# Squares of two feature blocks added on Pool ahead of the product with ones, in a norm of a two-layer decoder kernel

## The chip, the cores and the metric

The kernel runs on the 8 cores of one Trainium2 chip as one program. Times are device microseconds (us) of the slowest core. Each pair of cores takes one of four prompt sequences: the even core takes the first half of its tokens and 64 sample tokens, the odd core the second half with a halo of 136 tokens. The two kinds run differently built programs, and an even core ends last.

## The reference

One inference step of a trunk of two layers, for 4 prompts of 2048 tokens and 32 samples of 8 tokens, model width 2048. Cut to what matters here:

```python
def rmsnorm(x, g):
    r = lax.rsqrt(jnp.mean(xf * xf, axis=-1, keepdims=True) + EPS)
    return (xf * r).astype(x.dtype) * g

for i in range(2):
    h = rmsnorm(x, norm_mix[i])
    # token mixer (layer 0: gated short convolution, layer 1: sliding window attention)
    # in parallel with cross-attention into 256 memory tokens
    x = x + concat([mixer(h), cross_attention(h, mk, mv)]) @ w_out[i]
    x = x + swiglu(rmsnorm(x, norm_ffn[i]), w_gate[i], w_up[i], w_down[i])
y = rmsnorm(x, norm_final)
```

The changed code is the sum of squares in `rmsnorm`, over the 2048 features of a token.

## The kernel before

Activations lie transposed in SBUF: features on the 128 partitions in 16 blocks c = 0 to 15, tokens along the free dimension, cut into three tiles of 288 to 400 tokens. `xT` (tensor sb_rx, f32) is the residual stream; sb_ra and sb_rb are two bf16 buffers, sb_rc is shared by slots and temporaries, sb_rs holds five weight slots, sb_rn the temporaries of norms.

A mean over features is a sum over partitions, so TensorE makes it. `Norm.square(c)` squares one block of one token tile on ScalarE into a bf16 buffer, and `Norm.ones` multiplies that buffer by a 128x128 matrix of ones (sb_onesb), summing over the 16 blocks in one PSUM bank. `root` makes the inverse root on ScalarE (Ln, Exp); `apply(c)` scales block c on VectorE (STT, line 445). Six square buffers rotate and the product of block c is issued at `stat(c + 3)`; the last four products come at c = 15.

Norms of `xT` run in these places. In `l0_first` (layer 0's first norm) `norm(0)` runs alone while `xT` arrives by DMA; `norm(1)` and `norm(2)` are lists of side work, of which `qm(ti)` issues 0, 4, 6 and 7 pieces behind its four groups h = 0 to 3 of 16 matmuls. In a `sweep` (in `pass2`, where a group has 6 matmuls, and in the last `down` of each FFN, where it has 8) each of 16 groups d of a token tile is followed by `add_x` (VectorE, line 439, PSUM into `xT`) and by `stat(d)`, and the 16 `apply` of the tile before (`pending`) run one behind each of d = 0 to 7 and two behind d = 8 to 11. There are four sweeps of three tiles. One more norm is that of the memory tokens (`mem0_norm`).

Every engine runs its instructions in the order in which the Python code emits them. Pool (GpSimd) issues the DMAs of all weights, in order of use: before item i of the program its loads are emitted as far as slots are free. Line 1295 makes the loads 2 to 8 wait for a part of `xT`, numbers 7 and 8 for the last quarter of tile 1:

```python
while qi < len(queue):
    ...
    if s.free >= i:
        break
    DMA("pool", [(v.ap, src)], xT.r((12, 16), TA[0] if qi < 7 else TA[1]) if 2 <= qi < 9 else [], v.r(), s.key)
```

Line 451 lets at most eight (`PQD`) of Pool's DMAs be in flight: each waits for the landing of the one eight before it. Pool also scales the softmax rows in attention (line 442).

Of the kernel before, what the change touches and what calls it, by code (L numbers as in the profile page):

```python
# [296 lines left out]
def build():  # L297
# [46 lines left out]
    RS = Reg(chip, "rs", 5 * 4096, gran=4096)  # L344
    RN = Reg(chip, "rn", 2 * 800 + 2 * 1600 + 1024, gran=32)
    RK = Reg(chip, "rk", 1664, gran=32)
# [12 lines left out]
    def half(odd):  # L359
# [9 lines left out]
        sq = [View(RN, 800 * i, (400,), BF16) for i in range(2)]  # L369
        sqf = sq + [View(RC, 15360 + 800 * i, (400,), BF16) for i in range(4)]  # L370
        sqx = sq + [View(RC, 800 * i, (400,), BF16) for i in range(4)]
        rr = [View(RN, 1600 + 1600 * i, (400,), F32) for i in range(2)]
# [12 lines left out]
        stg0 = [View(RC, o, (256,), F32) for o in (23552, 24576, 9664)]  # L385
        sqm = sq + [View(RC, 27648 + 800 * i, (400,), BF16) for i in range(2)]
        sg = [View(RC, 1600 * i, (400,), F32) for i in range(2)]
        hmem1 = View(RA, 26752, (16, 256), BF16)
        mstage = [View(RA, 34944 + 1024 * i, (256,), F32) for i in range(2)]
        stg1 = [View(RC, 7424 + 1024 * i, (256,), F32) for i in range(3)]  # L390
        NB = 8 + odd
# [88 lines left out]
        common = [Slot(RS, 4096 * i, "w%d" % i) for i in range(5)]  # L480
        xslots = [Slot(RC, o, "w%d" % (5 + i if i < 4 else 23)) for i, o in enumerate((3328, 15360, 19456, 23552, 27648))]
        aslots = [Slot(RA, 4096 * i, "w%d" % (9 + i)) for i in range(6)]
# [26 lines left out]
        class Norm:  # L509
            def __init__(self, src, gi, dst, a, b, bufs=sqx):  # L510
                self.src, self.gi, self.dst, self.a, self.b, self.n = src, gi, dst, a, b, b - a
                self.bufs, self.lag = bufs, len(bufs) // 2
                self.q = []
                self.bt = None
                self.k = None

            def square(self, c):
                if self.bt is None:
                    self.bt, self.br = bank("N")
                s = self.bufs[nsq[0] % len(self.bufs)]  # L520
                nsq[0] += 1
                ACTF(s.ap[:, :self.n], self.src.ap[:, c, self.a:self.b], AF.Square, self.src.r(c, (self.a, self.b)), s.r((0, self.n)))
                self.q.append((c, s))

            def ones(self):
                c, s = self.q.pop(0)
                MM(self.bt[:, :self.n], onesb[:], s.ap[:, :self.n], c == 0, c == 15, s.r((0, self.n)) + ["onesb"], [self.br])

            def stat(self, c):
                self.square(c)  # L530
                while len(self.q) > (self.lag if c < 15 else 0):
                    self.ones()

# [274 lines left out]
        def l0_first(slots):  # L808
# [4 lines left out]
            def norm(ti):  # L813
                nm = Norm(xT, 0, bigA, TA[ti][0], TA[ti][1], sqf)
                side.extend([lambda c=c: nm.stat(c) for c in range(16)] + [lambda: nm.root(next_rr())] + [lambda c=c: nm.apply(c) for c in range(16)])
# [132 lines left out]
        def mem0_norm(_):  # L948
            nm = Norm(memT, 5, hmem0, 0, 256, sqm)
            side.extend([lambda c=c: nm.stat(c) for c in range(16)] + [lambda: nm.root(rmem)] + [lambda c=c: nm.apply(c) for c in range(16)])  # L950
            rate[0] = 3
# [495 lines left out]
```

How the kernel before makes its waits and increments, by code:

```python
    def run(self, eng_name, eh, esem, dsem):  # L97
        ops = self.ops
        waited = {}
        for o in ops:
            if o["eng"] != eng_name:
                continue
            need = {}
            for j in o["deps"]:
                p = ops[j]
                key = ("d", p["dma"]) if p["dma"] is not None else ("e", p["eng"])
                if p["sv"] > need.get(key, 0):
                    need[key] = p["sv"]
            for key, v in need.items():
                if waited.get(key, 0) >= v:
                    continue
                waited[key] = v
                sem = dsem[key[1]] if key[0] == "d" else esem[key[1]]
                eh.wait_ge(sem, v)
            if o["fn"] is None:
                continue
            ins = o["fn"](eh)
            if o["dma"] is not None:
                if not isinstance(ins, (list, tuple)):
                    ins = [ins]
                assert len(ins) == o["ndma"], (len(ins), o["ndma"])
                for x in ins:
                    x.then_inc(dsem[o["dma"]], 16)
            elif o["sig"]:
                ins.then_inc(esem[eng_name], 1)
```

## Time and profile before

| | |
|---|---|
| median of 3 runs | 2915.32 us (2914.01 to 2915.5) |
| the profiled execution | 2913.25 us |
| its span, slowest core (core 2) | 2911.7 us |
| spans of the even cores | 2909.0 to 2911.7 us |
| spans of the odd cores | 2867.1 to 2871.7 us |
| TensorE busy | 2829.2 us (97%), 18868 matmuls |
| VectorE, ScalarE, Pool busy | 952.7, 510.9, 396.0 us |
| granted TensorE clock | 0.993 of full speed |

A matmul's record lasts longer than its turn: in a full queue one of 368 columns starts every 0.156 us, while its row says 0.32. The busy share of an engine is a mean over stages, so the rows further down are taken from the stages in which a norm runs.

### The profile page before, as it was taken

How to read it: one execution, taken by the hardware profiler on the slowest of the kernel's cores; microseconds unless marked ns; L12 is line 12 of the kernel's file. 1: busy time of each engine (PE TensorE's matmuls, PEld its weight loads, DVE VectorE, ACT ScalarE, POOL GpSimd, SP SyncE). 2: the span in 40 equal slices, each digit the busy share in tenths (PEclk: the TensorE clock that was granted, in tenths of full speed). 3: DMA queues.
4: the chain of work that ended last, by engine and by line, in shares of the span. 5: the costliest groups of instructions: out<-in, count | busy, mean ns of one | idle time of the engine just before them, and what ended most of it. 6: DMA issues, size and time to landing. Idle time of an engine off the chain costs nothing.

```text
span 2911.7 us, 51081 instructions; the slowest of 8 cores (2867.1 to 2911.7 us)
## 1 busy us (share of the span) xinstructions
PE 2829.2 (97%) x18868; PEld 1780.1 (61%) x18868; DVE 952.7 (33%) x2004; ACT 510.9 (18%) x1410; POOL 396.0 (14%) x700
## 2 busy tenths in 40 slices
PE   6999999999999999999999899999999999999997
PEld 3665666666666666666656545566666666666664
DVE  2425436331302113131162568544131221312116
ACT  3213203100010000000133666220000000000013
POOL 0013111000000100001002667100000010000100
PEclk9999999999999999999999999999999999999999
DMA  8485447344352642525324412734317254252513
GB/s 191 90 131 84 74 69 123 73 81 89 83 100 51 122 75 51 90 41 102 51 44 82 81 31 46 122 59 87 73 21 122 48 93 70 42 101 44 102 30 124
DMA packets 79768, 232.59 MB, mean 80 GB/s; under 512 B 10208, under 2 KB 25184, under 8 KB 79488
## 3 DMA queue, kind: packets, MB, share of 16 engines
q0 software_dynamic: 60912, 204.83, 40.3%
q1 hardware_dynamic: 18608, 24.42, 2.7%
q8 instruction: 160, 2.62, 0.4%
q14 instruction: 88, 0.72, 0.1%
HBM read 424.86 MB, written 11.12 MB: 150 GB/s over the span
## 4 chain that ended last, share of the span: by engine, by line
PE 92%; DVE 2%; issue 2%; ACT 1%; POOL 1%; DMA 1%; SPq 1%; DVEq 0%; ACTq 0%; POOLq 0%
PE bank L430 91%; POOL sb_rc L442 1%; ACT sb_rc L436 1%; DMA sb_rx<-xe 1%; PE bank L433 1%; SPq L453 1%; DVE sb_st L605 0%; DVE bank L601 0%; DVE sb_st L651 0%; DVE sb_rx L439 0%; DVE sb_rc L445 0%; DVE sb_rx L445 0%; DVE sb_rc L439 0%; ACT sb_rn L436 0%; DVE sb_rc L459 0%
## 5 line engine op out<-in xcount | busy, mean ns | idle before, releaser
L430 PE MATMUL bank<-sb_ra,sb_rs 128*128 128x368 bf16 (+2 forms) x4672 | 807.8, 320 | 3.1 <-DVE sb_ra L445 2.0
L430 PE MATMUL bank<-sb_rb,sb_rs 128*128 128x368 bf16 (+3 forms) x4176 | 711.8, 317 | 3.6 <-ACT sb_ra L436 3.1
L430 PEld LDWEIGHTS bank<-sb_ra,sb_rs 128*128 128x128 bf16 x4672 | 453.3, 98 | 267.2 <-issue 20.1
L430 PEld LDWEIGHTS bank<-sb_rb,sb_rs 128*128 128x128 bf16 x4176 | 402.7, 98 | 234.1 <-issue 12.4
L439 DVE TENSOR_TENSOR sb_rx<-sb_rx,bank 128x368 f32<-128x368 f32 (+3 forms) x768 | 406.7, 531 | 416.0 <-PE bank L430 407.3
L436 ACT ACTIVATE sb_rc<-bank 128x368 f32<-128x368 f32 (+7 forms) x346 | 157.6, 456 | 1815.6 <-PE bank L430 1811.8
L430 PE MATMUL bank<-sb_rb,sb_rc 128*128 128x368 bf16 (+3 forms) x2576 | 441.6, 318 | 0.0
L430 PE MATMUL bank<-sb_ra,sb_rc 128*128 128x368 bf16 (+2 forms) x2304 | 403.3, 316 | 0.0
L430 PEld LDWEIGHTS bank<-sb_rb,sb_rc 128*128 128x128 bf16 x2576 | 251.9, 98 | 145.4
L430 PEld LDWEIGHTS bank<-sb_ra,sb_rc 128*128 128x128 bf16 x2304 | 225.4, 98 | 126.4
L439 DVE TENSOR_TENSOR sb_rb<-sb_rc,bank 128x368 bf16<-128x368 f32 (+2 forms) x180 | 91.0, 506 | 591.2 <-PE bank L430 589.6
L439 DVE TENSOR_TENSOR sb_ra<-sb_rc,bank 128x368 bf16<-128x368 f32 x132 | 70.2, 532 | 579.0 <-PE bank L430 579.0
L430 PE MATMUL bank<-sb_ra,sb_rb 128*128 128x368 bf16 (+1 forms) x1536 | 243.8, 317 | 0.0
L430 PEld LDWEIGHTS bank<-sb_ra,sb_rb 128*128 128x128 bf16 x1536 | 150.2, 98 | 85.5
L442 POOL TENSOR_SCALAR sb_rc<-sb_rc,sb_st 128x128 bf16<-128x128 bf16 (+2 forms) x256 | 167.9, 670 | 131.6 <-DVE sb_st L462 101.2
L430 PE MATMUL bank<-sb_ra 128*128 128x368 bf16 (+1 forms) x576 | 135.5, 317 | 0.0
L436 ACT ACTIVATE sb_rc<-bank,sb_st 128x129 bf16<-128x129 f32 (+2 forms) x288 | 115.0, 399 | 88.8 <-DVE sb_st L462 28.0
L430 PE MATMUL bank<-sb_rb,sb_ra 128*128 128x368 bf16 (+1 forms) x768 | 124.8, 317 | 0.0
L436 ACT ACTIVATE sb_rc<-sb_rx 128x368 bf16<-128x368 f32 (+3 forms) x160 | 78.4, 503 | 198.1 <-DVE sb_rx L439 182.3
L453 POOL DMA_DIRECT2D sb_rs<-w_gate x40 | 21.3, 532 | 652.1 <-PE bank L430 647.5
L430 PE MATMUL bank<-sb_rb 128*128 128x368 bf16 (+3 forms) x480 | 105.1, 317 | 0.0
L430 PEld LDWEIGHTS bank<-sb_rb,sb_ra 128*128 128x128 bf16 x768 | 75.1, 98 | 42.6
(107 smaller groups left out, 1298.0 us busy)
## 6 DMA issues: line engine op xcount, KB each, us to landing
sb_rc<-w_up POOLq DMA_DIRECT2D x43, 512.0 KB, 7.4
sb_rs<-w_down POOLq DMA_DIRECT2D x42, 512.0 KB, 6.2
sb_rs<-w_gate POOLq DMA_DIRECT2D x40, 512.0 KB, 6.9
sb_rs<-conv_w_in POOLq DMA_DIRECT2D x36, 512.0 KB, 6.4
sb_rc<-w_gate POOLq DMA_DIRECT2D x31, 512.0 KB, 6.1
sb_rs<-w_up POOLq DMA_DIRECT2D x28, 512.0 KB, 8.5
sb_rc<-w_down POOLq DMA_DIRECT2D x24, 512.0 KB, 6.8
sb_rs<-w_out_a POOLq DMA_DIRECT2D x32, 320.0 KB, 4.1
```

The lines of the kernel that those rows point to most:

```text
L430: P.op("pe", lambda e: e.matmul(out, lhsT=lhsT, rhs=rhs, start=start, stop=stop), r=r, w=w)
L433: P.op("pe", lambda e: e.transpose(out=out, in_=in_, identity=idn), r=r, w=w)
L436: P.op("act", lambda e: e.activation(out=out, in_=in_, func=func, **kw), r=r, w=w)
L439: P.op(eng, lambda e: e.tensor_tensor(out=out, in0=in0, in1=in1, op=op), r=r, w=w)
L442: P.op(eng, lambda e: e.tensor_scalar(out=out, in0=in0, scalar1=s1, scalar2=None, op0=op0), r=r, w=w)
L453: P.op(eng, lambda e: [e.dma_start(out=o, in_=i) for o, i in pairs], r=r, w=w, dma=key, ndma=len(pairs))
```

## The change

For a norm with `pairs` (all but `norm(0)` and the memory tokens' norm: 14 token tiles), blocks 0 to 13 are squared into f32 buffers, Pool adds two of them and rounds the sum to one of two bf16 buffers, and TensorE multiplies that. Blocks 14 and 15 go as before: 9 products instead of 16. The product of blocks (c - 1, c) is issued at `stat(c + 2)`; the last three come at c = 15. There are four f32 buffers instead of six bf16 ones. `norm(0)` keeps 16 products with a lag of two instead of three. One weight slot and the staging buffers of layer 1's memory keys and values (two instead of three, on odd cores) move in sb_rc.

```diff
-        sqf = sq + [View(RC, 15360 + 800 * i, (400,), BF16) for i in range(4)]
-        sqx = sq + [View(RC, 800 * i, (400,), BF16) for i in range(4)]
+        wide = lambda base: [(View(reg, o, (400,), F32), View(reg, o, (400,), BF16)) for reg, o in [(RN, 5824)] + [(RC, base + 1600 * i) for i in range(3)]]
+        sqf, sqx = wide(11264), wide(0)
...
-        stg1 = [View(RC, 7424 + 1024 * i, (256,), F32) for i in range(3)]
+        stg1 = [View(RC, 8896 + 1024 * i, (256,), F32) for i in range(2)]
...
-            def __init__(self, src, gi, dst, a, b, bufs=sqx):
+            def __init__(self, src, gi, dst, a, b, bufs=sqx, pairs=True):
...
-                self.bufs, self.lag = bufs, len(bufs) // 2
+                self.bufs, self.pairs = bufs, pairs
+                self.lag = len(bufs) - 1 if pairs else len(bufs) // 2
...
-                s = self.bufs[nsq[0] % len(self.bufs)]
+                wide, s = self.bufs[nsq[0] % len(self.bufs)]
                 nsq[0] += 1
-                ACTF(s.ap[:, :self.n], self.src.ap[:, c, self.a:self.b], AF.Square, self.src.r(c, (self.a, self.b)), s.r((0, self.n)))
-                self.q.append((c, s))
-
-            def ones(self):
+                n = self.n
+                pair = self.pairs and c < 14
+                q = wide if pair else s
+                ACTF(q.ap[:, :n], self.src.ap[:, c, self.a:self.b], AF.Square, self.src.r(c, (self.a, self.b)), q.r((0, n)))
+                if not pair:
+                    self.q.append((c, s))
+                elif c % 2 == 0:
+                    self.even = wide
+                else:
+                    v = self.even
+                    h = sq[(c // 2) % 2]
+                    TT("pool", h.ap[:, :n], v.ap[:, :n], q.ap[:, :n], ALU.add, v.r((0, n)) + q.r((0, n)), h.r((0, n)))
+                    self.q.append((c - 1, h))
+
+            def ones(self, last):
                 c, s = self.q.pop(0)
-                MM(self.bt[:, :self.n], onesb[:], s.ap[:, :self.n], c == 0, c == 15, s.r((0, self.n)) + ["onesb"], [self.br])
+                MM(self.bt[:, :self.n], onesb[:], s.ap[:, :self.n], self.n_ones == 0, last and not self.q, s.r((0, self.n)) + ["onesb"], [self.br])
+                self.n_ones += 1
 
             def stat(self, c):
                 self.square(c)
-                while len(self.q) > (self.lag if c < 15 else 0):
-                    self.ones()
+                while self.q and (c == 15 or self.q[0][0] <= c - self.lag):
+                    self.ones(c == 15)
...
-                nm = Norm(xT, 0, bigA, TA[ti][0], TA[ti][1], sqf)
+                nm = Norm(xT, 0, bigA, TA[ti][0], TA[ti][1], sqf, ti > 0)
```

On TensorE, in `qm(1)` of `l0_first` on an even core: the groups h = 0 and 1 (x32), the side work of `norm(2)` behind h = 1, group h = 2 (x16), and the side work behind it. Rows from sb_onesb are the products with ones; minus is the kernel before, plus the changed one.

```order
 L430 MATMUL bank<-sb_ra,sb_rs 128x368 x32
-L430 MATMUL bank<-sb_rc,sb_onesb 128x352
+L430 MATMUL bank<-sb_rn,sb_onesb 128x352
 L430 MATMUL bank<-sb_ra,sb_rs 128x368 x16
-L430 MATMUL bank<-sb_rc,sb_onesb 128x352 x3
-L430 MATMUL bank<-sb_rn,sb_onesb 128x352 x2
-L430 MATMUL bank<-sb_rc,sb_onesb 128x352
+L430 MATMUL bank<-sb_rn,sb_onesb 128x352 x3
 L430 MATMUL bank<-sb_ra,sb_rs 128x368 x16
```

Behind h = 1 one product stands as before, now of a pair (its buffer in sb_rn is written by Pool); behind h = 2 there are three instead of six.

On Pool, at the program's start on an even core: the last four of the first nine weight loads, and what follows them.

```order
 L453 DMA sb_rb<-conv_w_in 128x2048 x2
 L453 DMA sb_rc<-conv_w_in 128x2048 x2
+L439 TENSOR_TENSOR sb_rn<-sb_rn,sb_rc 128x368
+L439 TENSOR_TENSOR sb_rn<-sb_rc 128x368
+L439 TENSOR_TENSOR sb_rn<-sb_rn,sb_rc 128x368
+L439 TENSOR_TENSOR sb_rn<-sb_rc 128x368
+L439 TENSOR_TENSOR sb_rn<-sb_rn,sb_rc 128x368
+L439 TENSOR_TENSOR sb_rn<-sb_rc 128x368
+L439 TENSOR_TENSOR sb_rn<-sb_rn,sb_rc 128x368
```

The seven additions of `norm(1)` stand behind the loads 7 and 8 (sb_rc<-conv_w_in).

On Pool, at layer 0's `pass2`, on an even core: two weight loads, the load of the mask that `pass2` issues first, and what follows.

```order
 L453 DMA sb_rs<-w_down 128x2048 x2
 L453 DMA sb_rk<-mask 128x512
+L439 TENSOR_TENSOR sb_rn<-sb_rn,sb_rc 128x368
+L439 TENSOR_TENSOR sb_rn<-sb_rc 128x368
+L439 TENSOR_TENSOR sb_rn<-sb_rn,sb_rc 128x368
```

The additions of the sweep's three tiles (21, of which three are shown) stand behind these loads.

## Rows read from the trace of the kernel before

**Rows 1.** The cores: span and mean granted clock, slowest even and odd.

```profile
core 1: 2871.7 us, clock 0.996
core 2: 2911.7 us, clock 0.993
```

**Rows 2.** The page's chain that ended last, by engine (core 2, as all below).

```profile
PE 92%; DVE 2%; issue 2%; ACT 1%; POOL 1%; DMA 1%; SPq 1%; DVEq 0%; ACTq 0%; POOLq 0%
```

**Rows 3.** Timeline, first tile of layer 0's pass2: start, duration, engine, operation [idle before].

```profile
459.45 3.90 PE L430 MATMUL bank<-sb_rb,sb_ra 128*128 128x368 bf16 x24
...
460.72 0.54 DVE L439 TENSOR_TENSOR sb_rx<-sb_rx,bank 128x368 f32<-128x368 f32 x1 [0.48 <-PE bank L430]
461.35 0.51 ACT L436 ACTIVATE sb_rc<-sb_rx 128x368 bf16<-128x368 f32 x1 [80.38 <-DVE sb_rx L439]
...
463.19 0.32 PE L430 MATMUL bank<-sb_rc,sb_onesb 128*128 128x368 bf16 x1
...
464.28 0.32 PE L430 MATMUL bank<-sb_rc,sb_onesb 128*128 128x368 bf16 x1
...
477.18 0.51 ACT L436 ACTIVATE sb_rn<-sb_rx 128x368 bf16<-128x368 f32 x1 [0.58 <-DVE sb_rx L439]
477.83 0.32 PE L430 MATMUL bank<-sb_rn,sb_onesb 128*128 128x368 bf16 x1 [0.77 <-ACT sb_rn L436]
```

**Rows 4.** Timeline of VectorE, second tile of the same sweep.

```profile
481.12 0.53 DVE L439 TENSOR_TENSOR sb_rx<-sb_rx,bank 128x368 f32<-128x368 f32 x1
...
482.08 0.53 DVE L439 TENSOR_TENSOR sb_rx<-sb_rx,bank 128x368 f32<-128x368 f32 x1
...
488.93 0.53 DVE L439 TENSOR_TENSOR sb_rx<-sb_rx,bank 128x368 f32<-128x368 f32 x1
...
490.40 0.53 DVE L439 TENSOR_TENSOR sb_rx<-sb_rx,bank 128x368 f32<-128x368 f32 x1
```

**Rows 5.** Groups by line and form: xcount | busy us, mean ns | idle before.

```profile
L442 POOL TENSOR_SCALAR sb_rc<-sb_rc,sb_st 128x128 bf16<-128x128 bf16 x192 | 112.4, 602 | 39.2 <-DVE sb_st L462 25.1 <-ACT sb_rc L436 11.2 <-DVE sb_rc L439 1.4
L442 POOL TENSOR_SCALAR sb_rc<-sb_rc,sb_st 128x256 bf16<-128x256 bf16 x48 | 44.6, 936 | 72.9 <-DVE sb_st L462 65.2 <-ACT sb_ra L436 3.9 <-ACT sb_rc L436 3.5
```

**Rows 6.** Timeline around norm(1) in l0_first.

```profile
38.90 0.48 ACT L436 ACTIVATE sb_rb<-bank 128x368 bf16<-128x368 f32 x1 [13.16 <-PE bank L430]
...
39.95 0.32 PE L430 MATMUL bank<-sb_rc,sb_onesb 128*128 128x368 bf16 x1 [1.14 <-ACT sb_rc L436]
...
50.20 1.06 POOL L453 DMA_DIRECT2D sb_rc<-conv_w_in  x2 [24.86 <-DMA sb_rx<-xe]
...
51.86 4.14 PE L430 MATMUL bank<-sb_ra,sb_rs 128*128 128x368 bf16 x16
```

**Rows 7.** Timeline around norm(2) in l0_first.

```profile
66.44 1.64 ACT L436 ACTIVATE sb_rc<-sb_rx 128x352 bf16<-128x352 f32 x4
67.08 0.31 PE L430 MATMUL bank<-sb_rc,sb_onesb 128*128 128x352 bf16 x1 [1.10 <-ACT sb_rc L436]
...
76.44 1.88 PE L430 MATMUL bank<-sb_ra,sb_rs 128*128 128x368 bf16 x11
```

**Rows 8.** Timelines of Pool and TensorE at layer 0's and layer 1's pass2.

```profile
468.82 0.53 POOL L453 DMA_DIRECT2D sb_rk<-mask  x1 [1.77 <-DMA sb_rc<-w_gate]
...
1861.43 1.06 POOL L453 DMA_DIRECT2D sb_rc<-w_down  x2
1861.85 0.32 PE L430 MATMUL bank<-sb_rc,sb_onesb 128*128 128x368 bf16 x1
```

**Rows 9.** Windows: start:end, us, busy PE, PEld, DVE, ACT, POOL, then PEclk.

```profile
53.00:54.00 1.00, 1.00 (x4) 0.45 (x3) 0.65 (x2) 0.25 (x1) 0.00 (x0) 0.50 1.01 304
...
55.00:56.00 1.00, 1.00 (x9) 0.59 (x7) 1.00 (x3) 0.00 (x0) 0.00 (x0) 1.00 1.06 228
```

**Rows 10.** Timeline, VectorE and Pool at the same time in attention.

```profile
225.64 0.70 DVE L442 TENSOR_SCALAR sb_rc<-sb_rc,sb_st 128x256 bf16<-128x256 bf16 x2
...
225.78 1.84 POOL L442 TENSOR_SCALAR sb_rc<-sb_rc,sb_st 128x256 bf16<-128x256 bf16 x2 [3.84 <-DVE sb_st L462]
```

More of the change, by code:

```diff
@@ L344, in build @@
     RS = Reg(chip, "rs", 5 * 4096, gran=4096)
-    RN = Reg(chip, "rn", 2 * 800 + 2 * 1600 + 1024, gran=32)
+    RN = Reg(chip, "rn", 2 * 800 + 2 * 1600 + 1024 + 1600, gran=32)
     RK = Reg(chip, "rk", 1664, gran=32)
@@ L385, in half @@
         stg0 = [View(RC, o, (256,), F32) for o in (23552, 24576, 9664)]
-        sqm = sq + [View(RC, 27648 + 800 * i, (400,), BF16) for i in range(2)]
+        sqm = [(None, v) for v in sq + [View(RC, 27648 + 800 * i, (400,), BF16) for i in range(2)]]
         sg = [View(RC, 1600 * i, (400,), F32) for i in range(2)]
@@ L480, in half @@
         common = [Slot(RS, 4096 * i, "w%d" % i) for i in range(5)]
-        xslots = [Slot(RC, o, "w%d" % (5 + i if i < 4 else 23)) for i, o in enumerate((3328, 15360, 19456, 23552, 27648))]
+        xslots = [Slot(RC, o, "w%d" % (5 + i if i < 4 else 23)) for i, o in enumerate((4800, 15360, 19456, 23552, 27648))]
         aslots = [Slot(RA, 4096 * i, "w%d" % (9 + i)) for i in range(6)]
@@ L509, in half @@
         class Norm:
-            def __init__(self, src, gi, dst, a, b, bufs=sqx):
+            def __init__(self, src, gi, dst, a, b, bufs=sqx, pairs=True):
                 self.src, self.gi, self.dst, self.a, self.b, self.n = src, gi, dst, a, b, b - a
-                self.bufs, self.lag = bufs, len(bufs) // 2
+                self.bufs, self.pairs = bufs, pairs
+                self.lag = len(bufs) - 1 if pairs else len(bufs) // 2
                 self.q = []
+                self.n_ones = 0
+                self.even = None
                 self.bt = None
@@ L948, in mem0_norm @@
         def mem0_norm(_):
-            nm = Norm(memT, 5, hmem0, 0, 256, sqm)
+            nm = Norm(memT, 5, hmem0, 0, 256, sqm, False)
             side.extend([lambda c=c: nm.stat(c) for c in range(16)] + [lambda: nm.root(rmem)] + [lambda c=c: nm.apply(c) for c in range(16)])
```

## Prediction

> **What bounds the kernel now.** I read the list of cores first: the even ones end some 40 us behind the odd ones [rows 1], so core 2 sets the time and nothing that only odd cores do (their two staging buffers instead of three) counts. The page's chain that ended last comes next: 92% of it is TensorE [rows 2]. A matmul less is thus worth its turn in the queue, unless TensorE was waiting there or has to wait instead. So the third view was the timeline of each stage in which a norm runs. A turn of 368 columns comes from the products with ones at 463.19 and 464.28 us [rows 3]: seven turns (one product, six matmuls of a group) in 1.09 us, 0.156 us each.
>
> The same rows give the chain from a group to its product. Group d = 0 takes the first six of the 24 turns from 459.45, its last turn over at 460.38, and its addition on VectorE starts at 460.72, or 0.34 later; in the middle of the tile it is nearer 0.30. The square starts 0.63 us behind the addition's start and takes 0.51; TensorE starts 0.14 us behind a square's end (477.18 + 0.51 to 477.83). From a group's last turn to its product: 0.30 + 0.63 + 0.51 + 0.14 = 1.6 us. Before, three groups and two products (3.1 us) cover that, and TensorE waits only at the tile's end, where the product of block 15 stands right behind its group: 0.77 us, the idle time in the last row of rows 3.
>
> **What is removed.** 14 tiles lose 7 products each, 98 x 0.156 = 15 us of turns. Not all of it is on the path. At a sweep tile's end two products stand between block 15's group and its own (12/13's sum, 14) where three stood, and the wait for square 15 grows by that turn: 6 turns count. In `l0_first` the end of norm(1) is set by squares that wait for `xT`, and the end of norm(2) by squares queued behind each other, so none counts. 12 tiles x 6 x 0.156 = 11.2 us is the most that can be had.
>
> **What an addition costs.** 98 additions of 368 f32 elements with two inputs are new on Pool, and no row shows one. From below: VectorE does such an addition in 0.53 to 0.54 us [rows 3, 4]. From above: Pool's own scaling takes 0.602 us for 128 columns and 0.936 for 256 [rows 5], 2.6 ns a column, so 0.936 + 112 x 0.0026 = 1.23 us for 368. I take D = 1.1 us, nearer the row of the engine that does it, and a little less, since that row reads a scalar for each partition too. The Trainium skill (GPSIMD Engine Reference, 3.1) gives 4497 ns for an f32 add of 2048 elements on GpSimd, about twice VectorE; scaled by length that would be an estimate of 0.8 us here, and the sum below would be about 29 instead of 40 us. No run here shows it.
>
> **The sweeps of six matmuls (pass2, twice three tiles).** The product of blocks (2k, 2k + 1) now stands two groups and one product behind group 2k + 1: 13 x 0.156 = 2.02 us. The chain is 0.30 + 0.63 + 0.51, 0.1 for Pool to take over, D, 0.14: 1.68 + D = 2.78 us. Short by 0.76 us at each pair. A wait at one pair lengthens the cover of the next, so two successive waits together make 0.76: 0.38 a pair, 2.7 for seven pairs, less 6 or 7 turns (1.0): +1.6 us for the first tile. In the second and third tile VectorE also applies the norm of the tile before: 0.96 us from one addition to the next with one apply between, 1.47 with two [rows 4]; an apply is thus 0.51 and `add_x` 0.45. TensorE's new period with its waits is (1.87 + 0.16 + 0.38) / 2 = 1.2 us, so in d = 8 to 11 VectorE falls back 4 x (1.47 - 1.2) = 1.1 us. Before, a cover of 3.1 for a chain of 1.6 took such a lag in; now there is no slack and it comes on top: 2.7 us a tile. Sum: 2 x 1.6 + 4 x 2.7 = +14 us.
>
> **The sweeps of eight (last down, twice three tiles).** Cover 17 x 0.156 = 2.65 us, chain 2.78: a wait of 0.07 a pair, 0.5 a tile, against 0.95 saved: -0.4. With VectorE's 1.47 against a period of 1.4 the second and third tiles save nearly nothing, and the last tile of the kernel, of 288 columns, has a cover of 17 x 0.122 = 2.1 and loses about 1. Together 0.
>
> **norm(1) in l0_first.** The change puts its seven additions behind the loads 7 and 8 in Pool's queue. These wait for the last quarter of `xT`'s tile 1 and are issued from 50.20 to 51.26 us [rows 6]. But the first product of norm(1) stands behind group h = 1, before h = 2: at 39.95 in the row. Its sum is now ready at 51.26 + 1.1 + 0.14 = 52.5. TensorE, in order, stands for 12.5 us, and the groups h = 2 and 3 that ran inside the wait for `xT` run after it. Step by step: group h = 2 from 52.65 to 55.15; the fourth addition waits for the buffer of the second product and for squares 6 and 7, done 56.5; group h = 3 from 56.8 to 59.3; then ScalarE's copy (0.48, as at 38.90), squares 10 and 11 until 60.65, the sixth addition until 61.85, squares 14 and 15 in the buffers it frees until 62.9, the last three products until 63.5. The next group started at 51.86: **+11.7 us**. Nothing behind takes it back, since from there TensorE is the chain.
>
> **norm(2).** Behind h = 1 TensorE waited 1.10 us for the copy and one square [rows 7]. Now it needs two squares and an addition: 66.44 + 0.91 + 0.1 + 1.05 + 0.14 = 68.6 instead of 67.08, +1.56. Behind h = 2 the fourth addition, held by the buffer of the second product, adds 0.6. Behind h = 3 squares 14 and 15 wait for the sixth addition, about 1.0. Sum +3.2 us (next group at 76.44 before).
>
> **Pool's queue at pass2.** Layer 0: the load of the mask is issued at 468.82 us, as it waits for a landing eight loads back, and ends at 469.35 [rows 8]; the first product of the sweep stood at 463.19 [rows 3]. Now 469.35 + 1.1 + 0.14 = 470.6: +7.1 us beyond the pair's usual wait of 0.3. Layer 1: the last load before the sweep ends at 1862.49; the first sum is ready at 1863.7, where the sweep's first product stood at 1861.85 [rows 8]: 1.9 us, beyond the usual wait +1.1. In the two last downs the queue is empty.
>
> **The clock.** After the wait for `xT` TensorE ran at half of its 2.4 GHz, over the window 53 to 54 and at full clock again from 55 [rows 9], and 16 matmuls took 4.14 us instead of 2.49 [rows 6]: 1.65 us. The two long new stalls (12.5 and 7 us) each bring such a stretch: 3.3.
>
> **Hidden at nothing.** Squares into f32 instead of bf16: ScalarE has time left, and its row hardly moves with the output's size. `norm(0)`'s shorter lag: it follows the arrival of `xT`. The moved slot: its load is issued in the same order.
>
> **Sum.** 14 + 0 + 11.7 + 3.2 + 7.1 + 1.1 + 3.3 = +40 us (the 11.2 us of removed turns are inside the tiles' balances). The rows' execution took 2913.25 us, 2.1 below the runs' median: 2953 for it, **2956 us** against the median. With D = 0.53 the pass2 chain is 2.21 and a pair's wait 0.1, so that tiles end near their old time but for VectorE's lag (+1 each for four): 3 - 5 (eight-deep sweeps) + 10.5 + 1.5 + 6.5 + 0.5 + 3.3 = +20, 2936 us. With D = 1.23: +45, 2960.
>
> **Rivals.**
> (a) *Pool's additions and VectorE's applies exclude each other.* Both read two SBUF operands; if one that has begun holds the other off, each addition in a second or third tile costs VectorE 1.1 - 0.45 = 0.65 us beyond what lies under `add_x`. In pass2 a pair then takes 2 x 0.96 + 0.65 = 2.57 us on VectorE against TensorE's 2.4, and 2 x 1.47 + 0.65 = 3.6 in d = 8 to 11: about 2.1 us a tile, four tiles; in the eight-deep sweeps only the two pairs with double applies, 1.3 a tile, four tiles. +14 us: 2970. Against it: scaling on VectorE (225.64 to 226.34) and on Pool (from 225.78) lay on each other and VectorE was not held for Pool's 0.92 [rows 10]. For it: those have one tensor input each, and no row has Pool beside an apply. The Trainium skill (SBUF — State Buffer, Who interferes with whom) says just this: a VectorE instruction with two SBUF inputs and a GpSimd one that reads SBUF lock each other out for the whole instruction. Chance 0.30.
> (b) *The additions are not held in the queue* (loads issue earlier, or TensorE has nothing to lose there): only the rate counts, 14 + about 5 for l0_first: 2934. The rows of the two loads speak against it. 0.08.
> (c) *An addition costs 0.55 us or less*, 2936, 0.08.
> (d) *The other side: additions fully hidden.* If D stays below 2.02 - 1.68 = 0.34 us and Pool's queue is free when a tile starts, 11.2 us are saved: 2904. It decides at that D; Pool's shortest arithmetic row is 0.6 us for a third of the columns. With its halfway cases 0.06.
> The forecast itself (2948 to 2964): 0.48.
>
> **Range and chances.** From (b) and (c), 2936, to beyond (a), 2974: it leaves out a little over one in ten. Two measurements of this kernel can be told apart by about 0.2%, 6 us; between no change and that lies only the halfway part of (d). Faster 0.04, same 0.03, slower 0.93.
>
> **What would show it.** Right: on core 2, TensorE's waits list Pool's sb_rn as releaser, the two longest about 12 and 7 us, in `l0_first` and at the first tile of layer 0's pass2; first tiles of pass2 with a short wait at most pairs; Pool's TENSOR_TENSOR rows 98 times near 1.1 us; 98 matmuls fewer. Applies that last or start longer beside Pool's additions than without would show (a). Additions well under 0.9 us would make pass2 too dear here; and if the first product of norm(1) is not 12 us late, the largest term falls.

## The result, and the profile after

The changed kernel takes 2970.26 and 2969.66 us; the kernel before took 2914.82 us (median, 2914.01 to 2915.5). The ratio is 1.0189, 95% interval 1.0165 to 1.0214. Executions in which one die was disturbed are left out here and below. The profiled execution is the one of 2970.26 us.

The list of cores, as [rows 1]:

```profile
core 2: 2964.8 us, clock 0.988
...
core 4: 2968.4 us, clock 0.987
```

The page's chain that ended last, as [rows 2]:

```profile
PE 86%; DVE 3%; issue 3%; POOL 3%; DMA 2%; ACT 2%; SPq 1%; DVEq 0%; ACTq 0%; POOLq 0%
```

TensorE's share fell from 92% to 86%, and Pool, which had 1%, has 3% (this chain is that of core 4, now the longest). For the rest I stay on core 2, since the rows of before are from there: its span grew by 53.1 us.

TensorE's waits for additions on core 2 (what it waited for: us in total, times, longest):

```profile
PE bank L430 <- POOL sb_rn L439: 55.9, 53, 11.1
```

This row is new. Its 55.9 us are about the whole loss, but not each of them is a loss: where TensorE waited for a square before, it now waits for an addition. So I went on stage by stage. This table is read from the timelines of core 2 in both traces; a norm tile ends where its last product with ones starts. Each stage is counted from the end of the one above it, the first from the start of the program.

| stage (core 2) | forecast, us | measured, us |
|---|---|---|
| `l0_first` to the end of norm(1) | +11.7, and 1.65 of clock | 51.60 to 65.81: +14.2 |
| to the end of norm(2) | +3.2 | +2.7 |
| to the memory norm's end | 0 | +2.5 |
| pass2, layer 0, first tile | +8.7, and 1.65 of clock | +10.2 |
| pass2, layer 0, 2nd and 3rd tile | +5.4 | +4.1, +4.5 |
| last down, layer 0, three tiles | 0 | -0.7, +1.2, +1.1 |
| pass2, layer 1, first tile | +2.7 | +2.1 |
| pass2, layer 1, 2nd and 3rd tile | +5.4 | +4.1, +4.4 |
| last down, layer 1, three tiles | 0 | -0.7, +1.0, +2.5 |
| sum | +40 | +53 |

The tiles of the sweeps cost the same on all four even cores, to within 0.2 us, but for the first of each pass2. `l0_first` does not: up to the end of norm(2) from that of norm(1) it is +2.7 on core 2, +2.8 on core 6, and +6.7 and +7.5 on cores 0 and 4.

Timeline around norm(1), as [rows 6]:

```profile
49.67 1.07 POOL L453 DMA_DIRECT2D sb_rc<-conv_w_in  x2 [23.33 <-DMA sb_rx<-xe]
...
50.74 0.99 POOL L439 TENSOR_TENSOR sb_rn<-sb_rn,sb_rc 128x368 bf16<-128x368 f32 x1
...
51.87 0.47 PE L430 MATMUL bank<-sb_rn,sb_onesb 128*128 128x368 bf16 x1 [11.13 <-POOL sb_rn L439]
...
52.13 5.11 PE L430 MATMUL bank<-sb_ra,sb_rs 128*128 128x368 bf16 x16
...
64.32 0.47 PE L430 MATMUL bank<-sb_rn,sb_onesb 128*128 128x368 bf16 x1 [2.52 <-POOL sb_rn L439]
```

The two loads end at 50.74, the addition starts in the same hundredth, and TensorE takes its product 0.14 us after the addition's end, having stood for 11.13 us. The 16 matmuls behind it take 5.11 us. The windows (start:end, us, busy PE, PEld, DVE, ACT, POOL, then PEclk, DMA) say why:

```profile
54.00:56.00 2.00, 2.00 (x8) 1.00 (x7) 0.00 (x0) 0.91 (x2) 0.01 (x1) 0.50 1.08 223
...
64.00:66.00 2.00, 1.22 (x4) 0.61 (x5) 0.00 (x0) 0.91 (x2) 1.10 (x2) 0.55 0.04 6
...
97.00:98.00 1.00, 1.00 (x5) 0.45 (x4) 1.00 (x4) 0.00 (x0) 0.00 (x0) 0.50 0.00 0
...
490.00:492.00 2.00, 1.89 (x7) 0.95 (x8) 0.00 (x0) 0.00 (x0) 0.88 (x1) 0.50 1.04 174
```

TensorE is at half of 2.4 GHz there, and again in norm(1)'s end with its waits, behind norm(2), and at the start of layer 0's pass2. The stretch behind norm(2) explains the 2.5 us up to the memory norm, and the clock also explains why norm(2) costs more on core 4. Windows on core 2, from the end of norm(1) to that of norm(2) and from there on:

```profile
65.81:93.19 27.38, 20.72 (x122) 12.06 (x121) 11.55 (x23) 9.62 (x22) 6.38 (x7) 0.94 0.01 1
93.19:98.30 5.11, 5.11 (x18) 2.50 (x17) 3.36 (x7) 0.96 (x2) 0.00 (x0) 0.50 0.00 0
```

and on core 4, from the end of norm(1) to that of norm(2):

```profile
65.83:96.46 30.63, 23.98 (x123) 13.23 (x121) 11.54 (x23) 9.62 (x22) 6.38 (x7) 0.83 0.00 1
```

Behind norm(2) TensorE works without a break at half clock for 5.1 us, which costs half of that, 2.5 us. Where it does not (run 1 below), the stage takes 48.09 us, as before. On core 4 the same work takes 3.25 us more than on core 2, and the granted clock is 0.83 instead of 0.94: 5.2 us of full clock lost against 1.6. The timeline of the start of layer 0's pass2, as [rows 8]:

```profile
488.45 0.53 POOL L453 DMA_DIRECT2D sb_rk<-mask  x1 [1.98 <-DMA sb_rc<-w_gate]
489.00 0.97 POOL L439 TENSOR_TENSOR sb_rn<-sb_rn,sb_rc 128x368 bf16<-128x368 f32 x1
...
490.11 0.47 PE L430 MATMUL bank<-sb_rn,sb_onesb 128*128 128x368 bf16 x1 [6.95 <-POOL sb_rn L439]
...
496.94 0.32 PE L430 MATMUL bank<-sb_rn,sb_onesb 128*128 128x368 bf16 x1 [0.58 <-POOL sb_rn L439]
...
499.03 0.32 PE L430 MATMUL bank<-sb_rn,sb_onesb 128*128 128x368 bf16 x1
```

The load of the mask holds the first addition, as forecast. After that every second pair waits, 0.53 to 0.58 us: a wait at one pair lengthens the cover of the next. (The cover of a product is the other work that TensorE has between the group and that product; the chain is the time from the group to the finished sum.)

Now VectorE and Pool in the second tile, where VectorE also applies the norm of the tile before. The applies before and now, VectorE's own additions `add_x` now, and Pool's additions, each with shortest, median and longest in ns:

```profile
L445 DVE SCALAR_TENSOR_TENSOR sb_rb<-sb_rx,sb_gvec,sb_rn x96: 578/592/602, 479.6 to 1521.5; 128x368 bf16<-128x368 f32 x64, 128x352 bf16<-128x352 f32 x32
```

```profile
L445 DVE SCALAR_TENSOR_TENSOR sb_rb<-sb_rx,sb_gvec,sb_rn x96: 575/590/1321, 509.2 to 1561.6; 128x368 bf16<-128x368 f32 x64, 128x352 bf16<-128x352 f32 x32
...
L439 DVE TENSOR_TENSOR sb_rx<-sb_rx,bank x768: 440/536/572, 407.4 to 2949.3; 128x368 f32<-128x368 f32 x120, 128x352 f32<-128x352 f32 x60, 128x400 f32<-128x400 f32 x8, 128x288 f32<-128x288 f32 x4
...
L439 POOL TENSOR_TENSOR sb_rn<-sb_rc x42: 794/965/1208, 51.7 to 2945.9; 128x368 bf16<-128x368 f32 x21, 128x352 bf16<-128x352 f32 x12, 128x400 bf16<-128x400 f32 x6, 128x288 bf16<-128x288 f32 x3
```

An addition on Pool takes 0.96 us, below my 1.1. Before, the longest apply of this group took 602 ns; now one takes 1321. `add_x`, which has one operand in PSUM, is not stretched: 572 ns at most, and 573 before. The timelines of both engines in that tile show where the applies stand:

```profile
517.93 0.59 DVE L445 SCALAR_TENSOR_TENSOR sb_rb<-sb_rx,sb_gvec,sb_rn 128x368 bf16<-128x368 f32 x1
...
519.12 1.62 DVE L445 SCALAR_TENSOR_TENSOR sb_rb<-sb_rx,sb_gvec,sb_rn 128x368 bf16<-128x368 f32 x2
...
521.12 1.10 DVE L445 SCALAR_TENSOR_TENSOR sb_rb<-sb_rx,sb_gvec,sb_rn 128x368 bf16<-128x368 f32 x2
...
522.59 1.40 DVE L445 SCALAR_TENSOR_TENSOR sb_rb<-sb_rx,sb_gvec,sb_rn 128x368 bf16<-128x368 f32 x2
...
524.36 1.10 DVE L445 SCALAR_TENSOR_TENSOR sb_rb<-sb_rx,sb_gvec,sb_rn 128x368 bf16<-128x368 f32 x2
...
518.87 0.96 POOL L439 TENSOR_TENSOR sb_rn<-sb_rc 128x368 bf16<-128x368 f32 x1 [1.71 <-ACT sb_rc L436]
522.12 0.96 POOL L439 TENSOR_TENSOR sb_rn<-sb_rn,sb_rc 128x368 bf16<-128x368 f32 x1 [2.28 <-ACT sb_rc L436]
525.19 1.10 POOL L439 TENSOR_TENSOR sb_rn<-sb_rc 128x368 bf16<-128x368 f32 x1 [2.11 <-ACT sb_rc L436]
```

A pair of applies takes 1.10 us where no addition runs until its last 0.10 us (521.12). It takes 1.62 and 1.40 where an addition had begun (518.87, 522.12). The third addition begins while a pair of applies still runs (524.36 to 525.46) and takes 1.10 instead of 0.96. Each seems to hold the other off. That is rival (a), and run 6 puts it to the test.

### The profile page after: what moved, and what is told of

The parts are those of the page before. It is cut to its first block, busy times and chain, and to the rows that moved or that the text cites. A ratio compares the mean times of both kernels' runs of the same rounds, so it can differ in the third digit from the quotient of the medians.

```text
span 2968.4 us, 51142 instructions; the slowest of 8 cores (2920.3 to 2968.4 us)
## 1 busy us (share of the span) xinstructions
PE 2832.4 (95%) x18770; PEld 1770.7 (60%) x18770; DVE 968.1 (33%) x2004; ACT 511.7 (17%) x1410; POOL 491.5 (17%) x798
## 4 chain that ended last, share of the span: by engine, by line
PE 86%; DVE 3%; issue 3%; POOL 3%; DMA 2%; ACT 2%; SPq 1%; DVEq 0%; ACTq 0%; POOLq 0%
PE bank L430 85%; ACT sb_rc L436 2%; POOL sb_rc L442 1%; POOL sb_rn L439 1%; DMA sb_rx<-xe 1%; DVE sb_rx L439 1%; DMA sb_rc<-w_gate 1%; PE bank L433 1%; SPq L453 1%; DVE sb_rx L445 0%; DVE sb_rb L445 0%; DVE sb_st L620 0%; DVE sb_ra L445 0%; DVE sb_st L666 0%; DMA sb_ra<-w_out_b 0%
## 5 line engine op out<-in xcount | busy, mean ns | idle before, releaser
L430 PE MATMUL bank<-sb_rn,sb_onesb 128*128 128x368 bf16 (+4 forms) x110 | 35.1, 325 | 76.9 <-POOL sb_rn L439 56.6
L436 ACT ACTIVATE sb_rc<-sb_rx 128x368 f32<-128x368 f32 (+4 forms) x180 | 88.6, 502 | 114.4 <-DVE sb_rx L439 111.3
```

The source lines that it names most:

```text
L430: P.op("pe", lambda e: e.matmul(out, lhsT=lhsT, rhs=rhs, start=start, stop=stop), r=r, w=w)
L436: P.op("act", lambda e: e.activation(out=out, in_=in_, func=func, **kw), r=r, w=w)
```

## Experiments

Theory M (mutual): the loss is Pool's queue, plus the pairs' short cover, plus applies and additions that hold each other off. Its rivals are named with each run. The profiled times are given where only one or two executions count.

**1. No pairs in `l0_first`.** Norms 1 and 2 go back to one product for each block.

```diff
-                nm = Norm(xT, 0, bigA, TA[ti][0], TA[ti][1], sqf, ti > 0)
+                nm = Norm(xT, 0, bigA, TA[ti][0], TA[ti][1], sqf, False)
```

> The changed kernel, but layer 0's first norm makes 16 products per tile again (no additions on Pool in norm(1) and norm(2), four buffers, lag 2); the other 12 tiles keep the additions. Theory (Pool's queue holds the additions of norm(1) behind two loads that wait for xT, norm(2) waits for copy, squares and additions in turn, and both stalls bring half-clock stretches): the two traces differ by 25 us at the end of the memory norm, 0.7 of it from before norm(1), so this kernel runs 22 to 25 us below the changed one, about 2946 us, ratio to before 1.0105. Rival (those stalls only stand where TensorE would have waited later anyway): under 8 us below, 2962 us or more.

Measured: 2950.43, 2946.74 and 2950.74 us, ratio to before 1.0119 (1.0097 to 1.0141). The gain over the changed kernel is 19 to 23 us, where I had expected 22 to 25: the 25 us of the expectation stand on core 4, and core 2 has 19.4. On core 2 norm(1) ends at 50.96 us, the memory norm at 124.96 instead of 143.82: all but 0.6 of the 19 us of `l0_first` are gone. At the end of the first tile of layer 0's pass2 16.5 of them are left: that stage takes 2.4 us more than in the changed kernel, with TensorE at half clock for 17 us of it instead of 10. TensorE still waits for the mask's load, now 6.3 us. Its waits on core 2:

```profile
PE bank L430 <- POOL sb_rn L439: 33.8, 48, 6.3
```

**2. The loads free of norm(1).** The changed kernel, with loads 7 and 8 waiting for `xT`'s tile 0 instead of tile 1. The order in the queue stays; only what the loads wait for is earlier.

```diff
-... xT.r((12, 16), TA[0] if qi < 7 else TA[1]) if 2 <= qi < 9 else [], ...
+... xT.r((12, 16), TA[0] if qi < 9 else TA[1]) if 2 <= qi < 9 else [], ...
```

> The changed kernel, but loads 7 and 8 wait for the last quarter of xT's tile 0 instead of tile 1, so that they are issued 24 us earlier and Pool reaches the additions of norm(1) before TensorE needs the first sum. Theory (Pool's queue holds them): TensorE's wait at the first product of norm(1) falls from 11.1 us to under 3; the end of norm(1), 14.3 us late in the changed kernel, comes about 1 us late plus what the two loads delay xT's arrival (0 to 6 us). Time 2956 to 2962 us. Rival (that wait is something else, such as ScalarE or xT itself): 2969 us as before, the first product still about 11 us late.

Measured: 2956.8 and 2962.07 us. Timeline around norm(1):

```profile
25.90 1.11 POOL L453 DMA_DIRECT2D sb_rc<-conv_w_in  x2
...
40.55 0.96 POOL L439 TENSOR_TENSOR sb_rn<-sb_rn,sb_rc 128x368 bf16<-128x368 f32 x1 [13.54 <-ACT sb_rc L436]
...
41.65 0.32 PE L430 MATMUL bank<-sb_rn,sb_onesb 128*128 128x368 bf16 x1 [2.62 <-POOL sb_rn L439]
```

The loads are issued 24 us earlier, the addition waits for ScalarE alone, and TensorE's wait falls from 11.13 to 2.62 us. norm(1) ends at 53.21, 12.6 us earlier than with the change as it was, and 12.0 of that is still there at the memory norm (131.79). So on core 2 12.6 of the 14.2 us are the queue and the slow clock behind its wait, and not the additions themselves. On the other even cores the first wait is 2.62 us too, but norm(1) ends at 56.6 to 57.7, only 6.4 to 9.2 us earlier. There the last squares wait for `xT`, as on core 0:

```profile
54.11 0.51 ACT L436 ACTIVATE sb_rn<-sb_rx 128x368 f32<-128x368 f32 x1 [1.63 <-DMA sb_rx<-xe]
```

Before, core 0 had its last squares from 49.04 on. The expectation had allowed for this: 0 to 6 us by which two loads issued earlier delay `xT`. So the run gives back 8 to 13 us of the time, and not on every core all of the term. That the loads are what delays `xT` is not shown by a run of its own.

**3. Also no pairs in the first tile of layer 0's pass2.** Run 1 with one edit more.

```diff
-                norms = [Norm(xT, 2 + l, M, a, b) for a, b in TL]
+                norms = [Norm(xT, 2 + l, M, a, b, pairs=l == 1 or i > 0) for i, (a, b) in enumerate(TL)]
```

> As the first kernel of this call (no additions in layer 0's first norm), and also none in the first tile of layer 0's pass2, whose additions stand on Pool behind the load of the mask and the loads before it. Theory (queue wait of 7.5 us, a half-clock stretch behind it, and too little cover at each pair): 8 to 9 us below the first kernel, about 2938 us, ratio 1.0078. Rival (the mask's wait is caught up later): under 3 us below it.

Measured: 2940.52 to 2941.1 us, ratio 1.0092 (1.0074 to 1.011), 8.5 us below run 1 in the mean. On core 2 the tile ends at 482.10 instead of 490.94.

**4. The mask's load behind the sweep.** The changed kernel, the load of the mask issued after layer 0's pass2 sweep instead of before it.

```diff
                 if l == 0:
                     DMA("pool", [(maskb.ap, ...)], [], maskb.r(), "maskb")
```

(the two lines moved down, behind the loop over the sweep's tiles)

> The changed kernel with the load of the mask (needed only in layer 1) issued after layer 0's pass2 sweep instead of before it. Theory: Pool's last load before the additions is then the second w_down, which ended 2.5 us before the mask's issue ended, so the wait at the sweep's first product falls from 7.5 to about 5 us and the time by 2 to 3 us, 2966 to 2968 us. Rival (the adds wait for squares or buffers): no change.

Measured: 2962.9 to 2965.42 us, ratio 1.0167 (1.0149 to 1.0185). Timeline:

```profile
480.20 0.53 POOL L453 DMA_DIRECT2D sb_rs<-w_down  x1 [2.03 <-ACT sb_rc L436]
...
480.75 0.97 POOL L439 TENSOR_TENSOR sb_rn<-sb_rn,sb_rc 128x368 bf16<-128x368 f32 x1
...
481.86 0.32 PE L430 MATMUL bank<-sb_rn,sb_onesb 128*128 128x368 bf16 x1 [1.23 <-POOL sb_rn L439]
```

The addition still starts in the hundredths behind a load, now `w_down`'s, but the wait falls from 6.95 to 1.23 us. I had expected a gain of 2 to 3 us and got 4 to 7. From TensorE's arrival at its first product to the end of the tile it took 24.3 us with the change and 16.7 here: 5.7 of those 7.6 us are the wait, and the rest is the half clock, which this trace no longer has there (windows, PEclk behind the busy times):

```profile
482.00:484.00 2.00, 2.00 (x13) 1.20 (x13) 0.54 (x1) 0.02 (x1) 0.96 (x1) 1.00 1.08 164
```

What I had missed is how much earlier `w_down`'s load is issued than the mask's was, and that the slow clock hung on it.

**5. The root in PSUM.** The lock should need two SBUF operands in the apply (`sb_rx` and the root `sb_rn`). Here the root stays in the bank of the norm, so that an apply has one tensor operand in SBUF and one in PSUM.

```diff
+                    ACTF(self.bt[:, :n], self.bt[:, :n], AF.Ln, [], [self.br], scale=1.0 / D, bias=EPS)
+                    ACTF(self.bt[:, :n], self.bt[:, :n], AF.Exp, [], [self.br], scale=-0.5)
+                    self.rt_ap, self.rt_r = self.bt[:, :n], [self.br]
...
-                STT(..., gvec[:, self.gi, c:c + 1], self.rt.ap[:, :n], ...)
+                STT(..., gvec[:, self.gi, c:c + 1], self.rt_ap, ...)
```

> The changed kernel, but for the norms of xT the inverse root stays in the norm's PSUM bank (Ln and Exp write there), so that each apply on VectorE reads one operand from SBUF and one from PSUM instead of two from SBUF. Theory (an apply and a Pool addition hold each other off): the longest applies fall from 1.35 us to about 0.65 or less, and the second and third tiles of the four sweeps gain 1.9 us each in the six-deep ones and 0.4 to 1.5 in the eight-deep ones, together 10 to 13 us: about 2958 us, ratio 1.0150. Rival (the waits are only the length of the chain from square to product): no change, 2970 us.

And the same edit on the kernel before, as its control:

> Control for the inverse root in PSUM: the same edit on the kernel before, which has no additions on Pool. Theory of mutual exclusion: no other Pool instruction runs beside an apply in a sweep, so nothing changes, 2912 to 2918 us. Rival (applies from PSUM are faster or slower by themselves): more than 4 us to either side.

Measured: 2967.01 and 2967.77 us on the changed kernel, and 2924.16 to 2926.09 on the one before, ratio 1.0037 (1.0022 to 1.0052), where I had expected no effect. The edit had a cost of its own. The helper counts the bank as both written and read by an apply, so that each apply waited for the one before it; a pair of them on the timeline of VectorE:

```profile
524.82 1.29 DVE L445 SCALAR_TENSOR_TENSOR sb_rb<-sb_rx,sb_gvec,bank 128x368 bf16<-128x368 f32 x2
```

1.29 us instead of 1.10. The longest apply of 368 columns did fall from 1354 to 600 ns, but the time can't be used. It was a miss of the edit, mended in the next pair of runs.

**6. The root in PSUM, applies independent.** As 5, but the applies name only a tag of the bank that they read.

```diff
+        w += ["rt" + x[2:] for x in w if x.startswith("ps")]
...
-                    self.rt_ap, self.rt_r = self.bt[:, :n], [self.br]
+                    self.rt_ap, self.rt_r = self.bt[:, :n], ["rt" + self.br[2:]]
```

> The changed kernel with the inverse root in PSUM, as in the earlier run, but without the wait of each apply for the apply before it (the bank has a second name that applies only read; in the earlier run a pair of applies took 1.29 instead of 1.10 us). Theory of mutual exclusion: the second and third tiles now gain about 1.9 us each in the six-deep sweeps and 0.5 to 1.5 in the eight-deep ones against the changed kernel: 22.7 us for the second tile of layer 0's pass2 becomes about 20.8, and the time 2958 to 2961 us. Rival: tiles as in the changed kernel, 2969 us.

Its control on the kernel before:

> The control with the same edit on the kernel before. If the 9 us of the earlier control came from the applies' waits for each other: 2912 to 2918 us now. Rival (a read from PSUM costs by itself): 2924 us again.

Measured: 2957.41, 2958.34 and 2961.8 us, ratio 1.0150 (1.0132 to 1.0167); the control 2912.67 to 2916.14 and once 2948.47, which its ratio of 1.0016 (0.9989 to 1.0043) counts in. So the edit by itself costs and brings nothing that can be told from zero. The same lines, and the same place in the second tile, on core 2 of the changed kernel with this edit:

```profile
L446 DVE SCALAR_TENSOR_TENSOR sb_rb<-sb_rx,sb_gvec,bank x96: 571/591/598, 512.4 to 1560.5; 128x368 bf16<-128x368 f32 x64, 128x352 bf16<-128x352 f32 x32
...
L440 POOL TENSOR_TENSOR sb_rn<-sb_rc x42: 794/962/1042, 51.7 to 2941.5; 128x368 bf16<-128x368 f32 x21, 128x352 bf16<-128x352 f32 x12, 128x400 bf16<-128x400 f32 x6, 128x288 bf16<-128x288 f32 x3
```

```profile
519.14 0.59 DVE L446 SCALAR_TENSOR_TENSOR sb_rb<-sb_rx,sb_gvec,bank 128x368 bf16<-128x368 f32 x1
...
524.81 1.10 DVE L446 SCALAR_TENSOR_TENSOR sb_rb<-sb_rx,sb_gvec,bank 128x368 bf16<-128x368 f32 x2
...
518.96 0.97 POOL L440 TENSOR_TENSOR sb_rn<-sb_rn,sb_rc 128x368 bf16<-128x368 f32 x1 [1.89 <-ACT sb_rc L437]
...
524.35 0.96 POOL L440 TENSOR_TENSOR sb_rn<-sb_rn,sb_rc 128x368 bf16<-128x368 f32 x1 [2.34 <-PE bank L431]
```

The applies at 519.14 and 524.81 overlap additions and take 0.59 us, and 1.10 for a pair: no apply is stretched any more. The second and third tiles, before / changed / this run:

| tile | before | changed | root in PSUM |
|---|---|---|---|
| pass2, layer 0 | 18.60, 17.79 | 22.71, 22.28 | 21.32, 21.03 |
| last down, layer 0 | 23.64, 22.67 | 24.82, 23.73 | 24.04, 23.07 |
| pass2, layer 1 | 18.54, 17.89 | 22.67, 22.27 | 21.49, 20.84 |
| last down, layer 1 | 25.52, 18.83 | 26.57, 21.30 | 25.55, 20.54 |

The lock is 8.5 us over these eight tiles. What is left in pass2 is +2.7 to +3.2 a tile. I had worked out 2.7 without a lock, but with D = 1.1; the same working with 0.96 gives about 2.4, so 0.3 to 0.8 us a tile has no account.

**7. Each addition twice.** In the 12 tiles of the sweeps, the same addition issued twice, so that its cost can be read by itself.

```diff
-                    TT("pool", h.ap[:, :n], v.ap[:, :n], q.ap[:, :n], ALU.add, ...)
+                    for _ in range(2 if self.gi else 1):
+                        TT("pool", h.ap[:, :n], v.ap[:, :n], q.ap[:, :n], ALU.add, ...)
```

> The changed kernel with each of Pool's additions issued twice in a row in the 12 tiles of the sweeps (same result). The chain from a group to its sum grows by 0.92 us. Theory (short cover, shared by two successive waits): first tiles grow by half of 0.92 for each of seven pairs, 3.2 us, in the six-deep sweeps, and by about 3 in the eight-deep ones where the addition was nearly covered; in the other tiles, where applies also stand still for the second addition, by 5 to 6 us each. Together 55 us, about 3024 us. Rival (a fixed handover costs, not the addition's length): under 20 us more, below 2990.

Measured: 3008.01 to 3016.66 us, ratio 1.0325 (1.0302 to 1.0347): some 40 us more, where I had expected 55. The waits, and the timeline of TensorE in the first tile of layer 0's pass2:

```profile
PE bank L430 <- POOL sb_rn L439: 103.4, 68, 13.5
```

```profile
500.33 0.32 PE L430 MATMUL bank<-sb_rn,sb_onesb 128*128 128x368 bf16 x1 [1.33 <-POOL sb_rn L439]
502.71 0.32 PE L430 MATMUL bank<-sb_rn,sb_onesb 128*128 128x368 bf16 x1 [0.20 <-POOL sb_rn L439]
506.18 0.32 PE L430 MATMUL bank<-sb_rn,sb_onesb 128*128 128x368 bf16 x1 [1.28 <-POOL sb_rn L439]
508.69 0.32 PE L430 MATMUL bank<-sb_rn,sb_onesb 128*128 128x368 bf16 x1 [0.32 <-POOL sb_rn L439]
```

Two pairs take 5.85 us (500.33 to 506.18) instead of 4.81 (496.94 to 501.75 with the change). An addition more (the two of a pair start 1.1 us apart) costs 1.04 in two pairs, or about half of itself in each: 84 x 0.5 = 42 us. TensorE pays half of the chain's growth, since one wait serves two pairs. Each of the 12 tiles grew, by 1.9 to 4.4 us and 43.5 in all (core 2), so the path goes through the additions in every sweep tile once they are longer. By the same rule 0.1 us more of duration would cost some 4 us of the kernel. A shorter addition need not give that back: the first tiles of the last downs are already 0.7 below before, of 0.94 that they can gain.

**8. Keep what pays.** The root in PSUM; no pairs in `l0_first` and in the first tile of layer 0's pass2; and a fifth buffer, so that a product with ones stands one group further behind its squares (lag 4).

```diff
-        sqf, sqx = wide(11264), wide(0)
+        sqf, sqx = wide((11264, 12864, 14464)), wide((0, 1600, 3200, 8896))
...
-                self.lag = len(bufs) - 1 if pairs else len(bufs) // 2
+                self.lag = len(bufs) - 1 if pairs else max(2, len(bufs) - 2)
```

> All causes taken away at once and the pairs kept: no additions in layer 0's first norm and in the first tile of layer 0's pass2, inverse root in PSUM, a fifth f32 buffer so that a pair's product comes one group later (cover 2.95 instead of 2.02 us for a chain of 1.68 + 0.96 = 2.64). Theory: 11 tiles save 6 turns of 0.156 us each, less 1 us of waits behind double applies in four tiles: 4 to 9 us below the kernel before, 2906 to 2911 us, ratio 0.9970 to 0.9985. Rival (there is a further cost of the additions that the account lacks): at or above 2915 us.

Measured: 2907.18 to 2912.12 us, ratio 0.9984 (0.9973 to 0.9996), 2 to 8 us below before. TensorE's waits for additions in the 11 tiles that keep pairs:

```profile
PE bank L431 <- POOL sb_rn L440: 8.3, 14, 0.8
```

The second and third tiles of pass2 take 18.77 and 18.25 us in layer 0: still 0.2 and 0.5 above before. In the second tile its waits stand at the two products behind the double applies, 0.62 and 0.77 us. The last downs take 22.70 and 22.01 in layer 0, 0.9 and 0.7 below.

**9. Pairs in the eight-deep sweeps alone.** As 8, with `pairs=False` for all of pass2.

> As the kernel above, but pairs only in the six tiles of the eight-deep sweeps (pass2 with 16 products, lag 3, five buffers). Theory: 6 tiles x 6 turns x 0.156 = 5.6 us below the kernel before, 2909 us, ratio 0.998. Rival (pairs cost even there): 2915 us or more.

Measured: 2908.48 to 2911.69 us, ratio 0.9986 (0.9977 to 0.9996). Counted on core 2, five of the six tiles of the last downs gain 0.9 to 1.1 us each over before, the short last one 0.1: 5.0 in all. Six turns of 0.156 are 0.94. Where the cover is long enough and nothing is locked, an addition costs nothing and the removed products are paid out in full.

Runs 8 and 9 beat the kernel before by 4 to 5 us in 2915, and both intervals lie below 1. Most of run 8's gain isn't in the norms. It is 5.8 us on core 2. But from the end of layer 0's last down to the end of the first tile of layer 1's pass2, a stretch that is nearly all attention, run 8 took 360.5 us there, run 9 363.5, before 364.2 and the changed kernel 366.3. That is 3.7 of the 5.8 us. These are the windows before and in run 8:

```profile
1512.43:1876.62 364.19, 341.10 (x2613) 201.96 (x2613) 199.28 (x504) 175.81 (x672) 185.02 (x317) 0.97 0.46 79
```

```profile
1511.55:1872.04 360.49, 336.09 (x2605) 199.91 (x2606) 199.13 (x504) 175.75 (x672) 192.02 (x324) 0.99 0.47 80
```

The granted clock goes with it: 24 us at half clock before, in three stretches, 20 us in run 9, and 10 us in run 8, in two. (The changed kernel has 24 us as before; its 2.1 us more are the first tile of pass2.) Even cores of one execution differ in this too. Whether the edit has a part in it, no run shows.

## Why the prediction was right, and where it was off

The forecast was 2956 us, 2936 to 2974, slower with a chance of 0.93; it came out at 2970. The direction and the largest terms held; the likeliest case did not. The case that happened is rival (a), priced at 2970 with a chance of 0.30.

That its price was hit to the microsecond is luck. It had 14 us for the lock (an apply and an addition holding each other off), and run 6 shows 8.5. Most of the rest came from the clock, which the forecast had too small: 2.5 us behind norm(2) and 0.8 more than forecast behind norm(1)'s stall on core 2, and 3.3 us more at norm(2) on core 4, which ended last.

- **norm(1) in `l0_first`, +11.7.** Right in mechanism: the addition stood behind loads 7 and 8 to the hundredth, the product started at 51.87 against the 52.5 forecast, and freeing the loads (run 2) gave 12.6 us back on core 2. With the clock it was 14.2 against 13.4; 1.1 of the 14.2 stood already at the end of norm(0), which moves by up to 1.1 us from run to run.
- **norm(2), +3.2.** Right in kind, and close on core 2: 2.7. In other executions of the same code it was +1.9 to +7.5, and the granted clock goes with it, so that one hit says little. Run 1 gave `l0_first` back, 18.9 us of the 19.4 lost.
- **Pool's queue at pass2, +7.1 and +1.1.** Right: the wait at the mask's load was 6.95 us, and layer 0's first tile took 10.2 more against the 10.3 of all its terms. Run 4 moved the additions behind another load, issued 8 us earlier, and the wait fell to 1.23 us.
- **An addition, 1.1 us.** Mis-sized by 0.14: 0.96 us. I had gone by the row of Pool's own scaling [rows 5], which also reads a scalar. The Trainium skill (GPSIMD Engine Reference, 3.1) had led to an estimate of 0.8 us; the measurement, 0.96, lies between the two and decides.
- **The sweeps of six.** The first tiles with their alternating waits were as worked out: at D = 0.96 the chain is 1.68 + 0.96 = 2.64, less the cover of 2.02: 0.62 for two pairs, and 0.53 to 0.58 in the rows. In the later tiles run 6 has 2.7 to 3.2 without the lock, where the working with 0.96 gives 2.4.
- **The step that was off most** is the one on VectorE's share in the second and third tiles, which left out that an apply and an addition hold each other off. I had rows 10 before me and read them as evidence against it: scaling on Pool beside scaling on VectorE, with no hold. But these have one tensor operand each, and an apply has two. The four later pass2 tiles cost 17.1 us and not 10.8, the six tiles of the last downs 4.4 and not 0; rival (a) had 19.2 and 5.2. Run 6 removed the lock by moving one operand to PSUM and took back 8.5 us. The Trainium skill (SBUF — State Buffer, Who interferes with whom) states that a VectorE instruction with two SBUF inputs contends with a GpSimd instruction that reads SBUF. The trace agrees: applies of up to 1354 ns with both operands in SBUF and of 598 at most with one in PSUM (128 x 368, run 6).
- **The clock, +3.3.** Right in kind, too small. The 1.65 us of a stretch was read from a record, 4.14 us, and a record is longer than its turns: from 51.86 to the next group at 55.84 it was 3.98, so 1.5. In the changed kernel the group behind norm(1)'s stall took 4.91 us from its start at 52.13 to the next product at 57.04, where 16 turns at full clock are 2.49: 2.4 us. The stall at the mask's load cost 1.9 (run 4), and the stretch behind norm(2), which had no term at all, 2.5. That is 6.8 on core 2 against 3.3.
- **Rival (d), fully hidden.** Wrong for this kernel, but the mechanism is real: run 9 shows the turns paid out, 5.0 us, where the cover is long and nothing is locked.

Left open: why the stretches at half clock in attention differ from run to run and from core to core; the 0.3 to 0.8 us a tile of pass2 that stay in run 6; and +1.7 us in the kernel's last tile there, of 288 columns, where I had put 1. In the rows shown an instruction that had begun ran on and the other one waited; more of the order in which the two go was not looked into.

## What to carry to other kernels

Before putting arithmetic on Pool, list what stands ahead of it in Pool's queue: a DMA whose buffer or source is late holds everything behind it, and an engine two steps on pays (11.1 and 7.0 us here, more than all the products removed). Then see what VectorE does at that time: here an instruction with two tensor operands in SBUF and Pool's addition held each other off, and leaving one operand in PSUM, where its sum stood anyway, took that away (8.5 us). Count a stretch of slow clock behind a long wait of TensorE, and look at more than one core before calling a stage's cost known: norm(2) cost 2.7 us on one and 7.5 on another. And compare the length of the chain with the work that covers it before counting what is removed: the six turns of a tile were paid out where the cover was long (run 9), and not where it was short.

## What the runs showed of the hardware beyond this

- Pool adds two f32 tiles of 128 x 368 into bf16 in 0.96 us, 0.79 for 288 columns and 1.03 for 400. VectorE's addition of 368 columns, which writes f32 and has one operand in PSUM, takes 0.53.
- The hold works both ways: applies of 0.59 us grew to 1.35, additions of 0.96 to 1.10 (of 400 columns, 1.03 to 1.21). With the PSUM operand neither grew: at most 0.60 for the applies of 368 columns and 0.98 for the additions (1.04 with 400).
- Behind the stalls of 11.1 and 7.0 us TensorE was granted 1.2 of its 2.4 GHz (0.50 in the windows from 54 to 56 and from 490 to 492 us), around norm(1)'s end from 64 to 66 nearly so (0.55), where it was busy 1.22 of 2 us, and from 93.19 to 98.30 behind norm(2)'s waits, where it was busy throughout.
- Loads issued 24 us earlier (run 2) went with a later `xT` on three of four even cores: its last squares of norm(1) on core 0 ran from 54.11 us, and from 49.04 before.
